# Dealing the stick-breaking heads between the forget-gate heads in a two-block transformer kernel

## The reference

```python
h = x @ w_in[i]
# per head: forget-gate attention (6 heads)
logits = q k^T * scale + c_q - c_k ; causal ; softmax ; @ v
# stick-breaking attention (5 heads)
z = q k^T * scale
log_not = where(strict, log_sigmoid(-z), 0)
after = reverse_cumsum(log_not) - log_not
a = where(strict, exp(log_sigmoid(z) + after), 0) ; @ v
# sparse attention (5 heads): softmax over the 64 best keys of an index score per query
score = sum_h iw_h * relu(iq_h ik^T) ; top_k(score, 64) ; softmax over these ; @ v
gates = sigmoid(g)                       # 3 x 1024 channels
merged = gates0 * (o_fox @ w_up_fox) + gates1 * (o_sb @ w_up_sb) + gates2 * (o_dsa @ w_up_dsa)
x = layer_norm(alpha * x + merged @ w_out)
x = layer_norm(alpha * x + mlp(x) + ple(x))
```

## Time and profile before

| | us |
|---|---|
| median of 3 runs | 1937.59 |
| lowest, highest | 1932.92, 1938.59 |
| span of the profiled execution | 1927.3 |
| TensorE busy in it | 1729.6 (90%) |
| VectorE busy | 871.0 (45%) |
| ScalarE busy | 458.2 (24%) |
| mean granted TensorE clock | 0.918 of full |

### The profile page before, as it was taken

One profiled execution on the slowest core, in us unless ns is written; L12 is line 12 of the kernel. 1 busy time (PEld: TensorE's weight loads), 2 busy tenths in 40 slices (PEclk: granted clock), 3 DMA queues, 4 the chain that ended last, 5 costly groups with the idle time before them and its releaser, 6 DMA issues. The chain is left out here.

```text
span 1927.3 us, 22021 instructions
## 1 busy us (share of the span) xinstructions
PE 1729.6 (90%) x8947; PEld 1315.0 (68%) x8947; DVE 871.0 (45%) x1318; ACT 458.2 (24%) x755; POOL 36.8 (2%) x59
## 2 busy tenths in 40 slices
PE   5897999999879996999988899994998998899995
PEld 1455879345569995767866599962776876489982
DVE  0543975223265551017655455534006664455536
ACT  2012232111144441002221244411002221144420
POOL 0002010000000000000000000000000000000000
PEclk9988989777789998999989899996998997999998
DMA  9321110222155505431322444413432231445520
GB/s 362 140 88 44 45 44 2 87 88 88 34 184 187 203 3 194 146 131 48 127 88 86 174 177 174 175 43 127 171 131 86 90 111 63 160 150 199 191 87 22
DMA packets 102155, 228.75 MB, mean 119 GB/s; under 512 B 5440, under 2 KB 13760, under 8 KB 101312
## 3 DMA queue, kind: packets, MB, share of 16 engines
q1 hardware_dynamic: 99056, 219.80, 32.0%
q10 hardware_dynamic: 3024, 7.90, 1.1%
HBM read 226.64 MB, written 1.05 MB: 118 GB/s over the span
## 5 line engine op out<-in xcount | busy, mean ns | idle before, releaser
L814 PE MATMUL psum<-xT,ring 128*128 128x256 f32 (+1 forms) x1504 | 332.6, 383 | 16.6 <-issue 16.6
L814 PEld LDWEIGHTS psum<-xT,ring 128*128 128x128 f32 (+1 forms) x1504 | 272.3, 184 | 68.5 <-issue 20.6
L586 PE MATMUL psum<-channels_rounded,work_rounded 128*128 128x256 f32 x1536 | 285.8, 286 | 2.6 <-DVE work_rounded L654 2.6
L623 DVE TENSOR_TENSOR work_rounded<-ring,work_rounded 128x1024 fp32r<-128x1024 f32 x192 | 222.3, 1220 | 103.0 <-ACT work_rounded L614 102.9
L597 PE MATMUL psum<-work_rounded 128*128 128x512 f32 x1152 | 265.7, 390 | 0.0
L586 PEld LDWEIGHTS psum<-channels_rounded,work_rounded 128*128 128x128 f32 x1536 | 245.7, 195 | 4.9 <-issue 4.1
L597 PEld LDWEIGHTS psum<-work_rounded 128*128 128x128 f32 x1152 | 214.7, 188 | 43.6
L614 ACT ACTIVATE work_rounded<-ring 128x1024 fp32r<-128x1024 f32 x192 | 187.1, 1046 | 175.4 <-PE psum L597 108.5
L586 PE MATMUL psum<-work_rounded 128*128 128x256 f32 x768 | 219.8, 286 | 0.0
L586 PEld LDWEIGHTS psum<-work_rounded 128*128 128x128 f32 x768 | 150.0, 195 | 0.8
L1497 PE MATMUL psum<-ring,small 128*2 128x512 f32 x192 | 98.3, 671 | 17.4 <-DMA ring<-in_w_mod 17.4
(11 more groups left out here) (352 smaller groups left out, 1949.0 us busy)
## 6 DMA issues: line engine op xcount, KB each, us to landing
ring<-in_w_in SPq DMA_DIRECT2D x22, 2048.0 KB, 9.0
ring<-in_w_ff SPq DMA_DIRECT2D x16, 2048.0 KB, 8.0
ring<-in_w_ff_in SPq DMA_DIRECT2D x16, 2048.0 KB, 7.8
ring<-in_w_ff_out SPq DMA_DIRECT2D x16, 2048.0 KB, 7.8
ring<-in_w_mod SPq DMA_DIRECT2D x12, 2048.0 KB, 7.9
ring<-in_w_out SPq DMA_DIRECT2D x6, 2048.0 KB, 8.2
ring<-in_w_up SPq DMA_DIRECT2D x4, 2048.0 KB, 8.0
ring<-in_w_ple_gate SPq DMA_DIRECT2D x4, 2048.0 KB, 7.9
```

What stands on the lines that cost most here:

```text
L586: mm = pe.matmul(psum[:, 4 + 2 * half + q, i * SEQ:(i + 1) * SEQ], w1[pw][:, k, m * P:(m + 1) * P], y[py][:, k, :], start=((k, n) == (0, 0 ...
L623: dve.tensor_tensor(parts.low[i % 2][:, at], ring[:, SLOT * (n % RING) + 1024 * c: SLOT * (n % RING) + 1024 * (c + 1)], exact(parts.high[i ...
L814: mm = pe.matmul(ps[base:base + m, at:at + SEQ], unit[:, k, col:col + m], yT8[:, k, :], start=(k == 0), stop=(k == KC - 1))
```

## The change

`HEADS` is dealt: fox0, sb0, fox1, sb1, fox2, sb2, fox3, sb3, fox4, sb4, fox5, and then the sparse heads.

```diff
-HEADS = [("fox", h) for h in range(6)] + [("sb", h) for h in range(5)] + [("dsa", h) for h in range(5)]
+HEADS = [(kind, h) for h in range(5) for kind in ("fox", "sb")] + [("fox", 5)] + [("dsa", h) for h in range(5)]
```

## The result

The changed kernel's median is 1945.56 us against 1936.32 us. One of its seven executions took 4371.70 us, in a slow state of the chip; the ratio and its 95% interval leave it out: 1.0042 (1.0028 to 1.0057), that is 5.4 to 11.0 us slower, most likely 8.1.

What follows compares the result with a forecast made beforehand. TensorE was taken to set the pace, losing time only where waits break its matmuls. New waits +3.5 less old waits 2.0 gave +1.5 us per layer, +3.0 in two: 1940.6 us (+0.15%), range 1935 to 1946.

Steps and rivals of the forecast that it cites:

- S, T, gate and V: TensorE's parts of a step: next head's scores, previous head's middle product, 32 gate matmuls (6.91 us), previous head's output (0.71).
- the odd steps: Steps 1, 3, 5, 7, 9, stick-breaking scores with a forget-gate head's products: no wait; present waits go, -2.0 us per layer.
- n = 8 and n = 10: Even attention steps without top-k: VectorE's chain ends at 8.46 us for n = 8, under TensorE's 9.97, so no wait.
- the chain of the top-k steps: Steps 2, 4, 6: VectorE's sequence lets V start at 11.07 us, not 9.97; three steps cost +3.5 us per layer.
- the four old waits: Waits of V for line 1282 at n = 7 to 10, 0.51 us each: their removal saves 2.0 us per layer.
- Line 1276 behind the top-k: VectorE's T addition placed after top-k: taken as 0.47 us, bounds zero and 0.55; six times, -2.8 to +0.5 us.
- The loads and the banks: Weight loads released by the same gate blocks and an unchanged bank sequence: costed at nothing.
- the step that held the clock at 1.00 between the gate blocks: Reasoning that TensorE's granted clock stays at its upper level, 2.4 GHz, throughout between the first and last gate block.
- 2 us each way for moved clock edges: Allowance for a shifted program moving clock changes either way, all of them together.
- a rival with a chance of 14%: Clock rival: over a microsecond of standstill in six steps drops the clock, 1.4 us each, 8.4 over forecast, 1949; 14%.
- Evening out: Rival: light scores beside heavy ones spread VectorE's work so no wait is left; 4.0 us faster, 1933.6; 10%.
- The forecast's own bounds: Whole kernel: 1935.8 to 1943.1 us around 1940.6, from the unknown cost of line 1276 and moved clock edges.

Runs made afterwards that it cites:

- the moved dealt kernel: Changed kernel with one dense product in gate block 0 repeated twice, so all later work comes 0.86 us later; ratio to before 1.0023 (1.0009 to 1.0036).
- The two ratios: Changed kernel against the kernel before, in the first comparison 1.0042 and, unedited, in a repeated one 1.0031 (1.0014 to 1.0048).
- the two kernels with the gate block split: Line 1282 early and the head's middle product between halves of the gate block: on the dealt order 1.0014, on the order of before 1.0008.

## Why the prediction was right and where it was wrong

*Right, to 0.01 or 0.02 us:* that TensorE's row of matmuls sets the pace and only line 1282 breaks it; the lengths of S, T, gate and V; the odd steps unhindered (8.84 and 8.85 us); n = 8 and n = 10 without a wait (10.67); the chain of the top-k steps, 11.06 us measured to V against 11.07; the four old waits gone; a sum of +1.50 us per layer, which stands bare in the moved dealt kernel. Line 1276 behind the top-k is 0.47 us, not the bound of 0.55. The loads and the banks cost nothing, as taken.

*Wrong:* the step that held the clock at 1.00 between the gate blocks. The sum had no term for a fall; there were only 2 us each way for moved clock edges, and a rival with a chance of 14% and a wrong cause. I tied that rival to the idle microsecond and argued against it from an idle period (1.51 us before line 1001) and from the dense gate blocks on either side. But a fall needs no idle time: it came behind the small matmuls of V and S, and the six waits of the moved dealt kernel, the very condition of the rival, passed at a clock of 1.00. Its price I took from line 586 as 1.4 us; it measured 1.68, of which 0.51 beyond the wait in a top-k step. Three falls, two in top-k steps and one outside, are 0.51 + 0.51 + 1.68 = 2.7 us, and with the 3.0 forecast 5.7; the steps show 5.6. The two ratios say 8.1 and 6.0 (5.4 to 11.0, 2.7 to 9.3). Since every fall also moves all that follows, a part may lie in tails and later stretches; that part is not settled, and the two kernels with the gate block split show that it can be as large as the falls.

*The other rivals.* Evening out, -4 us: refuted, the wait is there when no fall swallows it. The Trainium skill's "TensorE: Matmul & The Clock Gate", section "A second HAM failure mode: psum-queue depth-cycling", says the clock can swing with brief idle spells between groups of matmuls. Here the clock did swing, but the measurements differ from that on the cause: with every wait removed there were four falls and six, and with all six waits in place, moved by 0.86 us, none. The Trainium skill's "Perfetto Trace Analysis", section "Optimization Strategy", suggests interleaving regimes with different busiest engines. Here TensorE was the busiest in both, so it is not the case of that page, and dealing the heads brought no gain (1.0042 and 1.0031).

*The baseline.* I took 10.3 us as lying around the span. It is 1.9 (1945.56 against 1943.7 for the profiled execution); the span shown of before, 1927.3, was simply that of a quick execution. The difference I forecast does not hang on it.

*What my range did.* The forecast's own bounds ended at 1943.1. The range held 1945.56 because it was widened by the spread of runs, not because I had the mechanism: that was luck. The 0.83 on "no change" was too much: the ratio came out at the edge of it, and a term for where clock edges fall should have given "slower" more.

## What to carry to other kernels

Where a row of matmuls repeats with a steady period, it may hold a high clock by its position alone; an edit that only shifts it lost that here in one layer of two. So count, beside waits, the stretches of small matmuls between dense blocks, and treat each as a possible fall with its own price (here 1.68 us). And removing waits of half a microsecond in one place can be worth nothing if later stages give it back: 4.1 us fewer between the gate blocks left the ratio at 1.0014. The waits of up to 2.4 us that recur in the tail, where the clock is already low, were worth more than all others here. Judge such edits by step lengths in two traces each, and by ratios of many executions, never by two spans, and do not expect the two to add up.

## What was not expected of the hardware

The clock fell from 2.4 to 1.2 GHz in the midst of matmuls with no idle time before, in one case behind 2.79 us of V and score matmuls (64 to 256 columns, partly on 64 or 6 rows), and came back by itself during the dense gate block. Waits of 0.95 us each, six of them, brought no fall. Whether it fell changed with a shift of 0.86 us (the dealt order: three falls unshifted, none shifted) or 1.73 us (the order of before: none, then one); each shift has one trace of two layers. In two traces of the same program the falls came in the same steps, although the first of these steps began 6.2 us earlier in one than in the other. Falls occurred with a DMA share of 1.05 and of 0.00.
